# Index queries for tokens 128 to 511 only, and head weights in the spare rows of the index key's weight unit

## What is computed

```
h = rmsnorm(x, attn_norm[0])
qa, ka, va, qb, kb, vb, qi, ki, wi = split(h @ w_in_even)    # last three: 16*64, 64 and 16 columns
dsa_attention(qb, kb, vb, qi.reshape(B, S, 16, 64), rmsnorm(ki, idx_k_norm), wi * 16 ** -0.5, ...)
```

## Time and profile before

| | |
|---|---|
| three runs, median | 2437.33 us (2435.81 to 2437.86) |
| profiled execution, first to last instruction | 2438.6 us |
| TensorE busy | 2412.6 us, 99% |
| VectorE busy | 1414.2 us, 58% |
| ScalarE busy | 1094.4 us, 45% |
| stretch from the first matmul of unit 1 to the end of unit 9 | 16.78 to 71.90 us |

### The profile page before, as it was taken

One profiled execution on the slowest core, in us unless ns is written; L12 is line 12 of the kernel. 1 busy time (PEld: TensorE's weight loads), 2 busy tenths in 40 slices (PEclk: granted clock), 3 DMA queues, 4 the chain that ended last, 5 costly groups with the idle time before them and its releaser, 6 DMA issues.

```text
span 2438.6 us, 31286 instructions
## 1 busy us (share of the span) xinstructions
PE 2412.6 (99%) x12374; PEld 1937.7 (79%) x12374; DVE 1414.2 (58%) x2297; ACT 1094.4 (45%) x1793; POOL 400.0 (16%) x311
## 2 busy tenths in 40 slices
PE   9999999999999999999999999999999999999998
PEld 6666678888877767888888778788888888888887
DVE  4687567858745446664667565555556434652543
ACT  4455554424434545442444366644446324441442
POOL 0000312202210001220221210012122213220221
PEclk9999999999999999999999999999999999999999
DMA  4122143444432214443342320021110333232231
GB/s 155 62 87 87 57 150 122 142 126 128 146 98 78 87 57 155 127 148 127 121 143 88 104 87 19 19 86 44 44 44 22 121 117 113 79 118 81 95 115 59
DMA packets 70225, 235.06 MB, mean 96 GB/s; under 512 B 8032, under 2 KB 10208, under 8 KB 69696
## 3 DMA queue, kind: packets, MB, share of 16 engines
q1 hardware_dynamic: 70080, 233.07, 29.7%
HBM read 226.14 MB, written 4.28 MB: 94 GB/s over the span
## 4 chain that ended last, share of the span: by engine, by line
PE 66%; DVE 2%; ACT 1%; issue 1%; DMA 1%; POOL 0%; SPq 0%; DVEq 0%; ACTq 0%
PE psum L450 17%; PE psum L452 17%; PE psum L451 17%; PE psum L2565 2%; PE psum L1089 1%; PE psum L1064 1%; PE psum L1108 1%; PE psum L1979 1%; PE psum L1980 1%; PE psum L1981 1%; PE psum L1239 1%; PE psum L1250 1%; PE psum L1262 1%; PE psum L2530 1%; PE psum L2531 1%
## 5 line engine op out<-in xcount | busy, mean ns | idle before, releaser
L450 PE MATMUL psum<-hH,wH 128*128 128x512 f32 x1912 | 774.2, 405 | 5.2 <-DVE hL L601 2.9
L452 PE MATMUL psum<-hH,wL 128*128 128x512 f32 x1912 | 748.5, 391 | 0.0
L451 PE MATMUL psum<-hL,wH 128*128 128x512 f32 x1912 | 747.1, 391 | 0.0
L437 DVE TENSOR_TENSOR wL<-raw,wH 128x1024 fp32r<-128x1024 f32 (+3 forms) x354 | 444.9, 1257 | 376.9 <-ACT wH L432 376.0
L432 ACT ACTIVATE wH<-raw 128x1024 fp32r<-128x1024 f32 (+3 forms) x354 | 364.0, 1029 | 525.7 <-PE psum L452 524.4
L450 PEld LDWEIGHTS psum<-hH,wH 128*128 128x128 f32 x1912 | 359.7, 188 | 108.0 <-issue 37.4
L452 PEld LDWEIGHTS psum<-hH,wL 128*128 128x128 f32 x1912 | 359.1, 188 | 78.6
L451 PEld LDWEIGHTS psum<-hL,wH 128*128 128x128 f32 x1912 | 360.3, 188 | 65.8 <-issue 1.0
L1813 POOL TENSOR_TENSOR sg<-sg,cv 128x512 f32<-128x512 f32 x66 | 95.1, 1441 | 695.9 <-ACT sg L1644 695.9
L450 PE MATMUL psum<-gH,wH 128*128 128x512 f32 x506 | 197.5, 390 | 0.0
L451 PE MATMUL psum<-gL,wH 128*128 128x512 f32 x506 | 196.9, 389 | 0.0
(11 more groups left out here) (386 smaller groups left out, 3535.4 us busy)
## 6 DMA issues: line engine op xcount, KB each, us to landing
raw<-in_up SPq DMA_DIRECT2D x132, 512.0 KB, 3.7
raw<-in_dn SPq DMA_DIRECT2D x48, 704.0 KB, 4.1
raw<-in_win SPq DMA_DIRECT2D x56, 512.0 KB, 3.7
mbuf<-in_wmod SPq DMA_DIRECT2D x48, 512.0 KB, 4.0
raw<-in_we SPq DMA_DIRECT2D x33, 512.0 KB, 3.7
raw<-in_wq SPq DMA_DIRECT2D x24, 512.0 KB, 3.7
tm<-toep SPq DMA_DIRECT2D x32, 256.0 KB, 4.3
raw<-in_wo SPq DMA_DIRECT2D x32, 256.0 KB, 2.6
```

Source lines behind the costliest of these rows:

```text
L437: ve.do.tensor_tensor(flat_of(wLb, n), flat_of(rawb, n), flat_of(wHb, n).bitcast(F), ALU.subtract).then_inc(*w_lo.up(n))
L450: pe.do.matmul(o, H[:, k, :], high(k), start=k == 0, stop=False)
L451: pe.do.matmul(o, H[:, k, :], low(k), start=False, stop=False)
L452: ins = pe.do.matmul(o, L[:, k, :], high(k), start=False, stop=k == kt - 1)
```

## The change

The query units multiply only the activations of tokens 128 to 511 (384 columns in place of 512), and their copies out of PSUM cover those columns. The separate unit `wi` is gone: unit `we` 0 now holds the key's 64 columns once, then the 16 columns of `wi`, then 48 columns of zeros, and its output has the key in partitions 0 to 63 and `wi` in 64 to 79. VectorE writes the key twice, once for each half of the partitions. All that hangs between ticks moves to other ticks, and the index items start at tick 72.

```diff
-    out += [("we", 0), ("wi", 0)] + [("we", 1 + n) for n in range(8)]
+    out += [("we", n) for n in range(9)]
...
+    late = slice(128, S)
+
+    def late_part(pe, o):
+
+        high, low, ready = norm_ready(pe, "attn0", (hH, hL))
+        return lambda k: high(k)[:, late], lambda k: low(k)[:, late], o[:, late], ready
...
-            self.bank = bank[u] if name in ("we", "wi") and u < 2 else bank[2 + u % 2]
+            self.bank = bank[u] if name == "we" and u < 2 else bank[2 + u % 2]
...
-            out_ = [("ticks", 80)]
+            out_ = [("ticks", 72)]
...
-                part = h_part(pe, f"attn{layer}", x.bank[0:16, :] if x.kind == "wi" else x.bank)
+                part = late_part(pe, x.bank) if x.kind == "qi" else h_part(pe, f"attn{layer}", x.bank)
...
-                if i == 3 and x.kind == "qi" and x.c == 0:
+                if i == 1 and x.kind == "qi" and x.c == 1:
                     pe_first_norm(pe)
-                if i == 3 and x.kind == "qi" and x.c == 1:
+                if i == 3 and x.kind == "qi" and x.c == 2:
                     pe_factor(pe, 0)
-                if i == 7 and x.kind == "qi" and x.c == 2:
+                if i == 7 and x.kind == "qi" and x.c == 4:
                     pe_index_key(pe)
...
-                    ac.do.activation(turned(qi(x.c)), in_blocks(x.bank), ACT.Copy).then_inc(*ev_a.up(x.n))
-                if x.c == 0:
+                    ac.do.activation(turned(qi(x.c)[:, late]), in_blocks(x.bank[:, late]), ACT.Copy).then_inc(*ev_a.up(x.n))
+                if x.c == 1:
                     ac_scale(ac, "attn0", S)
-                elif x.c == 2:
+                elif x.c == 4:
                     ac_index_key(ac)
...
-                    ve.do.tensor_copy(turned(qi(x.c)), in_blocks(x.bank)).then_inc(*ev_v.up(x.n))
-                if x.c == 0:
+                    ve.do.tensor_copy(turned(qi(x.c)[:, late]), in_blocks(x.bank[:, late])).then_inc(*ev_v.up(x.n))
+                if x.c == 1:
                     ve_index_factors(ve)
-                elif x.c == 1:
+                elif x.c == 2:
                     ve_factor(ve, 0)
-                elif x.c == 2:
+                elif x.c == 4:
                     ve_index_key(ve)
...
-            if x.kind == "qi" and x.c == 1:
+            if x.kind == "qi" and x.c == 2:
                 sp_table(sp)
...
-            ins = pe.do.transpose(bank[5][:, i * 16:i * 16 + 16], wit[0:16, i * 128:i * 128 + 128],
-                                  C("ident", 0, 16)[0:16, :])
+            ins = pe.do.transpose(bank[5][:, i * 16:i * 16 + 16], wit[64:80, i * 128:i * 128 + 128],
+                                  C("ident", 64, 80)[64:80, :])
...
-        ve.do.tensor_tensor(kiT, bank[0], rs[:], ALU.mult).then_inc(*ev_v.up(k))
-        ve.wait_ge(*gemm.at(w))
-        ve.do.scalar_tensor_tensor(hf[0][0:16, :], bank[1][0:16, :], 0.25, rs[0:16, :], ALU.mult,
-                                   ALU.mult).then_inc(*ev_v.up((w, "w")))
+        ve.do.tensor_tensor(kiT[0:64, :], bank[0][0:64, :], rs[0:64, :], ALU.mult).then_inc(*ev_v.up((k, "k")))
+        ve.do.tensor_tensor(kiT[64:128, :], bank[0][0:64, :], rs[0:64, :], ALU.mult).then_inc(*ev_v.up((k, "k2")))
+        ve.do.scalar_tensor_tensor(hf[0][64:80, :], bank[0][64:80, :], 0.25, rs[64:80, :], ALU.mult,
+                                   ALU.mult).then_inc(*ev_v.up((k, "w")))
```

More of the change, by code:

```diff
@@ L94, in weight_units @@
     return out
-KTS = {"we": 8, "wi": 8, "wq1": 8, "win": 8, "wbr": 4, "wout": 8}
+KTS = {"we": 8, "wq1": 8, "win": 8, "wbr": 4, "wout": 8}
 for _l in range(3):
@@ L391, in size @@
     def size(n):
-        name = units[n][0]
-        return KTS[name], (16 if name == "wi" else 128)
+        return KTS[units[n][0]], 128
     apart = {at["up2", 22]: 0, at["up2", 1]: 1, at["up2", 23]: 2}
@@ L705, in __init__ @@
             self.name, self.index = name, index
-            self.bank = bank[u] if name in ("we", "wi") and u < 2 else bank[2 + u % 2]
+            self.bank = bank[u] if name == "we" and u < 2 else bank[2 + u % 2]
             self.ticks = KTS[name]
     def layer_units(layer):
-        names = [("we", 0, "ki", 0), ("wi", 0, "wi", 0)] + [("we", 1 + c, "qi", c) for c in range(8)] if layer == 0 else []
+        names = [("we", 0, "ki", 0)] + [("we", 1 + c, "qi", c) for c in range(8)] if layer == 0 else []
         for p in range(8):
@@ L723, in evicted @@
     def evicted(x):
-        if x.kind in ("ki", "wi", "q", "k") or x.kind == "qi" and x.c % 2 == 0:
+        if x.kind == "ki":
+            return ev_v.at((x.n, "w"))
+        if x.kind in ("q", "k") or x.kind == "qi" and x.c % 2 == 0:
             return ev_v.at(x.n)
@@ L835, in ac_fill @@
                 elif x.c == 0 and layer == 0:
-                    ac.wait_ge(*ev_v.at((at["wi", 0], "w")))
+                    ac.wait_ge(*ev_v.at((at["we", 0], "w")))
                 ac.do.activation(hf[x.c % 2][:], x.bank, ACT.Copy).then_inc(*ev_a.up(x.n))
@@ L910, in pe_index_key @@
         pe.do.matmul(bank[6], C("blk"), sq[0][:], start=True, stop=True).then_inc(*ik_mm.up(0))
-        pe.wait_ge(*ev_v.at(at["wi", 0]))
+        pe.wait_ge(*ev_v.at((at["we", 0], "t")))
         pe.wait_ge(*tab_v.at(1))
         for i in range(4):
-            ins = pe.do.transpose(bank[5][:, i * 16:i * 16 + 16], wit[0:16, i * 128:i * 128 + 128],
-                                  C("ident", 0, 16)[0:16, :])
+            ins = pe.do.transpose(bank[5][:, i * 16:i * 16 + 16], wit[64:80, i * 128:i * 128 + 128],
+                                  C("ident", 64, 80)[64:80, :])
         ins.then_inc(*ik_t.up(0))
     def ac_index_key(ac):
-        ac.wait_ge(*ev_v.at(at["we", 0]))
+        ac.wait_ge(*ev_v.at((at["we", 0], "k2")))
         ac.wait_ge(*tot.at("attn0"))
@@ L929, in ve_index_factors @@
         ve_table(ve)
-        w, k = at["wi", 0], at["we", 0]
+        k = at["we", 0]
         ve.wait_ge(*rs_s.at("attn0"))
         ve.wait_ge(*gemm.at(k))
-        ve.do.tensor_tensor(kiT, bank[0], rs[:], ALU.mult).then_inc(*ev_v.up(k))
-        ve.wait_ge(*gemm.at(w))
-        ve.do.scalar_tensor_tensor(hf[0][0:16, :], bank[1][0:16, :], 0.25, rs[0:16, :], ALU.mult,
-                                   ALU.mult).then_inc(*ev_v.up((w, "w")))
-        ve.wait_ge(*ev_v.at((w, "w")))
-        ve.do.tensor_tensor(turned(wit[0:16, :]), in_blocks(hf[0][0:16, :]), in_blocks(rs[0:16, :]),
-                            ALU.mult).then_inc(*ev_v.up(w))
+        ve.do.tensor_tensor(kiT[0:64, :], bank[0][0:64, :], rs[0:64, :], ALU.mult).then_inc(*ev_v.up((k, "k")))
+        ve.do.tensor_tensor(kiT[64:128, :], bank[0][0:64, :], rs[0:64, :], ALU.mult).then_inc(*ev_v.up((k, "k2")))
+        ve.do.scalar_tensor_tensor(hf[0][64:80, :], bank[0][64:80, :], 0.25, rs[64:80, :], ALU.mult,
+                                   ALU.mult).then_inc(*ev_v.up((k, "w")))
+        ve.wait_ge(*ev_v.at((k, "w")))
+        ve.do.tensor_tensor(turned(wit[64:80, :]), in_blocks(hf[0][64:80, :]), in_blocks(rs[64:80, :]),
+                            ALU.mult).then_inc(*ev_v.up((k, "t")))
     def ve_index_key(ve):
         ve.wait_ge(*ik_rs.at(0))
-        ve.wait_ge(*ev_v.at(at["we", 0]))
+        ve.wait_ge(*ev_v.at((at["we", 0], "k2")))
         ve.do.scalar_tensor_tensor(kiT, kiT, M("idxk"), ssum[:], ALU.mult, ALU.mult).then_inc(*ik_k.up(0))
@@ L3182, in lay @@
     we = g["w_in_even"][0]
-    o["we"] = np.concatenate([pack(np.concatenate([we[:, 4096:4160], we[:, 4096:4160]], 1)), pack(we[:, 3072:4096]),
-                              pack(we[:, :3072])], 0)
-    o["wi"] = np.ascontiguousarray(we[:, 4160:4176].reshape(8, 128, 16).transpose(1, 0, 2)).reshape(1, 128, 128)
+    o["we"] = np.concatenate([pack(np.concatenate([we[:, 4096:4176], np.zeros((D, 48), np.float32)], 1)),
+                              pack(we[:, 3072:4096]), pack(we[:, :3072])], 0)
     o["wq1"] = pack(g["w_in_odd"][0])
```

## The result

| | before | after |
|---|---|---|
| median of the runs | 2437.22 us (4 runs, 2435.81 to 2437.86) | 2421.47 us (4 runs, 2421.16 to 2423.57) |
| ratio, 95% interval | | 0.9937 [0.9923, 0.9951] |
| span of the profiled execution | 2438.6 us | 2420.0 us |
| first matmul of unit 1 to index item 0 | 16.78 to 72.67: 55.89 us | 15.92 to 56.00: 40.08 us |

The kernel is 15.75 us faster by the medians; 15.7 were forecast. The same pair measured once more (experiment 12) gave 2437.01 us (9 runs) and 2422.95 us (5 runs): 14.06 us, ratio 0.9941 [0.9929, 0.9954]. Each interval reaches some 3 us to either side, so the medians give the gain to a few us and no better; the distance in the last row is the closer measure, and experiment 9 shows what it leaves out.

A forecast was written before the change was run, and what follows sets the result against it. TensorE was taken to bound the stage by how many matmuls it issues and the distance between starts. 5.57 + 10.2 - 0.1 = 15.7 us off the median 2437.33 gave 2421.6 us, range 2420.0 to 2424.6.

The forecast's parts named there:

- TensorE bounds the stage, so its time goes through to the end: Unit 1 to the end of the query units: TensorE has no gap, so a microsecond saved reaches the kernel's end.
- The unit of head weights, 5.57 us: TensorE's separate unit of 24 matmuls goes, its columns ride in unit 0 at no cost: gain 5.57 us.
- The query units, 10.2 us by the middle of two neighbours: 192 query matmuls at 384 columns: 0.1733 us each, midway between 512 and 256 columns, gain 10.2 us.
- the rival that took it for one: Query matmuls: the 188 ns weight load is a floor at 384 columns, gain there 7.4, 2424.4 us; chance 6%.
- What hangs between the ticks costs what it did: Work on TensorE moved to other ticks: first norm 3.86 us, key's sums and transposes 1.30 us, both unchanged.
- The squares: Before the first norm: last square done at 20.3 us, TensorE asks at 22.0, 1.7 us after.
- `rs`: Norm's factor from ScalarE, in unit 3: ready at 30.95 us, asked for at 31.1; 0.1 us allowed, at most 0.5.
- The second copy: VectorE's extra write of the key, about 0.7 us: free by nearly 3 us before TensorE wants unit 5.
- The start: Unit 1's larger weights: VectorE's remainder done about 14.6 us, TensorE wants it at 16.78, covered by 2.2 us.
- The forecast's second rival: Larger first transfers delay the squares, TensorE waits at the first norm: gain 12 to 14, about 2424.5 us; chance 6%.
- The span: Whole profiled execution: 2438.6 - 15.7 = 2422.9 us, the old span taken as 1.3 above the median.

The follow-up runs named there:

- experiment 12: The changed kernel with nothing altered, measured again on one chip with the kernel before: 2422.95 us against 2437.01, ratio 0.9941.
- experiment 9: The kernel before with nothing altered, profiled a second time: span 2434.0 us, unit 1 to index item 0 55.88 us.
- experiment 4: The changed kernel with VectorE writing the key's second copy four times in place of once: 2422.55 us, ratio 0.9938.

## Why the prediction was right

- *TensorE bounds the stage, so its time goes through to the end.* Right. 15.81 us by the distance, 15.75 by the medians, and none of the lead at index item 0 given back in 2400 us. That the medians hit 15.7 so closely is luck in part: the same pair gave 14.06 the second time, and the forecast had nothing for the start, which takes 1.2 us or a little more when the clock is up.
- *The unit of head weights, 5.57 us.* Measured alone, 5.58.
- *The query units, 10.2 us by the middle of two neighbours.* Measured alone, 10.27, at 0.1733 us a matmul. The recorded length of a weight load (188 ns) was no bound; the rival that took it for one is excluded by 256 columns at 0.120.
- *What hangs between the ticks costs what it did.* 3.85 and 1.29 us against 3.86 and 1.30.
- *The squares.* Asked for 1.7 us after they are done, I wrote. That reading was wrong: the first ones-matmul takes VectorE's sum, which is ready 0.66 us before the last square, and the last square is asked for 1.7 us later still. By my own figures the margin would have been 2.4 us; it was 0.85. Two terms were off. Unit 1 began at 15.92 and not at 16.78, because the clock rose earlier in that execution; and I let the squares begin 1.2 us later, but missed that VectorE's remainders stand behind its own wait for `sm` in its order: the adds began at 16.43, and the last square was done 0.7 us later than forecast. My row of before could not show this wait, since there the constants had landed in time, but the code did.
- *`rs`.* Forecast level with its asking, 0.1 us; measured ready 0.24 us before the transposes start, no wait recorded.
- *The second copy.* Free within 0.1 us, by experiment 4.
- *The start.* Here the forecast was wrong, and the time did not show it. It had the remainder of unit 1 done at 14.6 and covered by 2.2 us; with the wait for `sm`, which the forecast itself put at 14.3, it would have had 15.5. Measured, it was done at 15.37 and asked for at 15.92, and was in time only because the clock was at half meanwhile; with the clock up unit 1 starts about 1.2 us later than the old one. The forecast's second rival, a late start, named the right neighbourhood and the wrong place: what comes late is VectorE's remainder of unit 1, behind the small constants, and neither the weights nor the squares.
- *The span.* Forecast 2422.9, seen 2420.0. I had taken 2438.6 for 1.3 above the median; the changed kernel's profiled execution took 2421.77 us with a span of 2420.0, and the second one of before 2435.84 with 2434.0, so the time is 1.8 above the span, and the first profile of before was an execution some 3 us slower than the median. The sum was right because it was added to the median.

## What to carry to other kernels

Where an engine is full, price an instruction by the distance between starts and interpolate between neighbours of the same form, not by its recorded duration. When such an engine's work shrinks, go through everything that it asks for on the way and subtract: here two margins of 6.7 and 5.4 us fell to 0.85 and 0.24, and each was shown to be that thin by asking earlier. Read in the code which instruction waits for what: the wait that did cost time, VectorE's for the small constants, could not be seen in the trace of before. And before a difference between two profiles is put down to the change, compare both at one instruction at a time and look at the granted clock: of 18.6 us, 0.9 at the start and 1.6 near 1393 us were the clock of those two executions.

## What had not been expected of the hardware

TensorE stands idle before the key's unit until the first `hL` is there. In the 11 profiles with three matmuls ahead, the granted clock then fell to half in 9, for 3.4 us in six and 6.8 us in three; these had stood 2.07 to 2.98 us. In the two where it did not fall (the second of before and experiment 4) TensorE had stood 1.93 and 1.85 us, and in the three kernels with five matmuls ahead, where it did not fall either, 0.85 to 1.52. The idle time thus separates the cases in these 14 profiles, but no run varied it alone, so no threshold follows from them. There is a second place: near 1367 to 1393 us TensorE waits 2.0 to 2.2 us in all 14 profiles, and in 7 of them the clock fell for 3.4 us, between 0.1 us before and 1.3 us after the end of that wait, in the same code, so there the length of the wait doesn't separate them. The 16-row unit cost 0.232 us a matmul, a little more than 128 rows (0.2267), though its weight loads were recorded at half the length (97 ns and 188).
